# Split operands in three passes for the attention scores of the third and fourth layer

## What is computed

```
# layer 3, per block of 128 queries
z = jnp.einsum('bhqd,bhkd->bhqk', qb, k).astype(jnp.float32) * scale
strict = kpos[None, :] < tpos[:, None]
...
# layer 4: queries and keys are normalised per head and scaled by a gain
k_sh = rms_norm(split_heads(kvf[..., :HD]), shared_k_norm_g)
...
q = rms_norm(split_heads(hn @ fox_w_q[j]), fox_q_norm_g[j])
...
logits = (jnp.einsum('bhqd,bhkd->bhqk', qb, k).astype(jnp.float32) * scale
          + fb[..., :, None] - f_cum[:, :, None, :])
causal = kpos[None, :] <= tpos[:, None]
```

## Time and profile before

| | us |
|---|---|
| median of 3 runs | 1357.53 |
| lowest and highest | 1356.75, 1357.81 |
| the profiled execution | 1357.98 |
| its span, first to last instruction | 1356.2 |
| busy in it: TensorE / VectorE / ScalarE | 1340.0 / 924.8 / 795.8 |
| mean granted TensorE clock | 1.0 of full speed |

### The profile page before, as it was taken

One profiled execution on the slowest core, in us unless ns is written; L12 is line 12 of the kernel. 1 busy time (PEld: TensorE's weight loads), 2 busy tenths in 40 slices (PEclk: granted clock), 3 DMA queues, 4 the chain that ended last, 5 costly groups with the idle time before them and its releaser, 6 DMA issues.

```text
span 1356.2 us, 21057 instructions
## 1 busy us (share of the span) xinstructions
PE 1340.0 (99%) x6920; PEld 1114.2 (82%) x6920; DVE 924.8 (68%) x1679; ACT 795.8 (59%) x1478; POOL 115.4 (9%) x182
## 2 busy tenths in 40 slices
PE   8999999999999999999999999999999999999998
PEld 7887888888888888888888888888887778888887
DVE  6877666556787766665687876666677877666665
ACT  7765655546765655554686665555478766555544
POOL 5220232300000000000000000000002210000000
PEclk9999999999999999999999999999999999999999
DMA  9444787765653555655644456555645545655551
GB/s 288 150 141 136 202 226 220 222 202 177 193 152 125 158 185 186 186 186 193 208 132 152 129 162 195 186 186 186 202 156 180 164 132 156 197 189 186 186 194 54
DMA packets 177851, 239.29 MB, mean 176 GB/s; under 512 B 13532, under 2 KB 152940, under 8 KB 177787
## 3 DMA queue, kind: packets, MB, share of 16 engines
q1 hardware_dynamic: 174778, 229.41, 53.3%
q0 software_dynamic: 2976, 9.02, 3.4%
q10 hardware_dynamic: 32, 0.01, 0.0%
HBM read 237.27 MB, written 1.13 MB: 176 GB/s over the span
## 4 chain that ended last, share of the span: by engine, by line
PE 93%; DVE 4%; DMA 1%; ACT 1%; issue 1%; POOL 1%; SPq 0%; DVEq 0%; POOLq 0%; ACTq 0%
PE acc L1289 17%; PE acc L1291 16%; PE acc L1290 16%; PE sc L1291 11%; PE sc L1289 11%; PE sc L1290 11%; PE turn L1411 6%; PE turn L1491 1%; DVE wlo L918 1%; PE sc L1446 1%; PE sc L1451 1%; DVE z L995 1%; PE turn L1475 1%; DMA bias<-nfc_scratch 0%; DMA raw<-in_da_w_qkv 0%
## 5 line engine op out<-in xcount | busy, mean ns | idle before, releaser
L918 DVE SCALAR_TENSOR_TENSOR wlo<-raw,gain,whi 128x512 fp32r<-128x512 f32 (+2 forms) x680 | 442.4, 707 | 25.2 <-ACT whi L680 25.1
L680 ACT ACTIVATE whi<-raw,gain 128x512 fp32r<-128x512 f32 (+2 forms) x680 | 418.9, 681 | 31.4 <-PE acc L1291 21.3
L1289 PE MATMUL acc<-whi,xhi 128*128 128x512 f32 (+1 forms) x704 | 255.4, 363 | 1.7 <-DVE wlo L918 1.6
L1289 PE MATMUL sc<-whi,xhi 128*128 128x512 f32 x640 | 253.0, 395 | 0.0
L1291 PE MATMUL sc<-whi,xlo 128*128 128x512 f32 x640 | 249.8, 390 | 0.0
L1290 PE MATMUL sc<-wlo,xhi 128*128 128x512 f32 x640 | 249.4, 390 | 0.0
L1291 PE MATMUL acc<-whi,xlo 128*128 128x512 f32 (+1 forms) x704 | 247.4, 351 | 0.0
L1290 PE MATMUL acc<-wlo,xhi 128*128 128x512 f32 (+1 forms) x704 | 247.2, 351 | 0.0
L1289 PEld LDWEIGHTS acc<-whi,xhi 128*128 128x128 f32 x704 | 133.1, 189 | 22.9 <-issue 3.2
L1291 PEld LDWEIGHTS acc<-whi,xlo 128*128 128x128 f32 x704 | 133.0, 189 | 18.3
L1290 PEld LDWEIGHTS acc<-wlo,xhi 128*128 128x128 f32 x704 | 133.3, 189 | 15.8
(11 more groups left out here) (179 smaller groups left out, 1557.0 us busy)
## 6 DMA issues: line engine op xcount, KB each, us to landing
raw<-in_ffn_w_gu SPq DMA_DIRECT2D x176, 256.0 KB
raw<-in_ffn_w_gate SPq DMA_DIRECT2D x88, 256.0 KB
raw<-in_ffn_w_up SPq DMA_DIRECT2D x88, 256.0 KB
raw<-in_ffn_w_down SPq DMA_DIRECT2D x44, 512.0 KB
raw<-in_ffn_w_d SPq DMA_DIRECT2D x44, 512.0 KB
raw<-in_ple_w_gate SPq DMA_DIRECT2D x32, 512.0 KB
raw<-in_da_w_qkv SPq DMA_DIRECT2D x32, 256.0 KB
raw<-in_na_w_qkv SPq DMA_DIRECT2D x32, 256.0 KB
```

Source lines behind the costliest of these rows:

```text
L680: ins = act.activation(whi[:, u % RING, c0:c1], raw[:, u % RING, c0:c1], ACT.Copy, scale=scale)
L918: ins = dve.scalar_tensor_tensor(out=lo, in0=w, scalar=gain[:, g:g + 1], in1=hi.bitcast(F32), op0=ALU.mult, op1=ALU.subtract)
L1289: pe.matmul(dst, xh, wh, start=first, stop=False)
```

## The change

Layers 3 and 4 take the way of layers 1 and 2. `split_scores` and `qk32` go, and ScalarE writes the upper halves into `qkT`. VectorE gets a new step `turnqk` in both layers, which makes the lower halves and releases the bank. In layer 4, where the gains of queries and keys are applied here, VectorE does this with four multiply-subtract operations of 128x256 per group instead of two subtractions of 128x512. The step stands ahead of the weight halves of its step in layer 3, and ahead of the value eviction in layer 4.

```diff
-    L_SB: [[], [], ["evacv", "scores0"], ["scores1"], ["post0", "post1"], ["turnp0"], ["turnp1"], ["pvt*"]],
-    L_FX: [["evacqk"], ["headnorm"], ["evacv"], ["mask", "scores0"], ["scores1", "post0"], ["turnp0", "post1"], ["turnp1"],
+    L_SB: [[], ["turnqk"], ["evacv", "scores0"], ["scores1"], ["post0", "post1"], ["turnp0"], ["turnp1"], ["pvt*"]],
+    L_FX: [["evacqk"], ["headnorm"], ["turnqk", "evacv"], ["mask", "scores0"], ["scores1", "post0"], ["turnp0", "post1"], ["turnp1"],
...
-SPLIT = count([x for x in EV_LIST if x[0] in ("x", "o", "g", "side") or x[0] == "qk" and split_scores(x[1])])
+SPLIT = count([x for x in EV_LIST if x[0] in ("x", "o", "g", "side", "qk")])
...
                 elif name == "turnqk":
-                    if L == 2 and j == 0:
-                        act.wait_ge(fin_ready, T)
...
                         dst = qkT[:, :, t * P:(t + 1) * P]
-                        if split_scores(L):
-                            act.activation(dst, src, ACT.Copy).then_inc(turn_hi, 1)
-                            continue
-                        dst = qk32[:, :, t * P:(t + 1) * P]
                         if L == L_FX:
                             act.activation(dst[:, 0:2], src[:, 0:2], ACT.Copy, scale=gain[:, GAIN_Q:GAIN_Q + 1])
-                            ins = act.activation(dst[:, 2:4], src[:, 2:4], ACT.Copy,
-                                                 scale=gain[:, GAIN_K:GAIN_K + 1])
+                            act.activation(dst[:, 2:4], src[:, 2:4], ACT.Copy, scale=gain[:, GAIN_K:GAIN_K + 1])\
+                                .then_inc(turn_hi, 1)
                         else:
-                            ins = act.activation(dst, src, ACT.Copy)
-                        ins.then_inc(turn_out[e % 2], 1)
+                            act.activation(dst, src, ACT.Copy).then_inc(turn_hi, 1)
...
-                        lo_half(("qk", L, j, t), qklo[at], qkT[at],
-                                tb[e % 2][:, :].rearrange("p (k c) -> p k c", k=4), e)
+                        src = tb[e % 2][:, :].rearrange("p (k c) -> p k c", k=4)
+                        if L != L_FX:
+                            lo_half(("qk", L, j, t), qklo[at], qkT[at], src, e)
+                            continue
+                        dve.wait_ge(turn_hi, SPLIT[("qk", L, j, t)])
+                        for b, g in ((0, GAIN_Q), (2, GAIN_K)):
+                            ins = dve.scalar_tensor_tensor(out=qklo[at][:, b:b + 2], in0=src[:, b:b + 2],
+                                                           scalar=gain[:, g:g + 1],
+                                                           in1=qkT[at][:, b:b + 2].bitcast(F32), op0=ALU.mult,
+                                                           op1=ALU.subtract)
+                        ins.then_inc(turn_out[e % 2], 1)
...
-                        if not split_scores(L):
-                            for q in range(2):
-                                ins = pe.matmul(dst[q], qk32[rows[q], b, tile], qk32[rows[q], 2 + b, 0:kk], start=True,
-                                                stop=True)
-                            continue
                         for n, (x, y) in enumerate(((qkT, qkT), (qkT, qklo), (qklo, qkT))):
```

More of the change, by code:

```diff
@@ L124, in keys @@
     return P if L >= L_SB and t == 0 else S
-def split_scores(L):
-    return L < L_SB
 def p_blocks(L, t):
@@ L257, in build @@
         fin_gain = sb("fin_gain", [P, D])
-        qk32 = fin_gain[:, :].rearrange("p (k c) -> p k c", k=4)
         ident = sb("ident", [P, P])
```

## The result

Over eight executions each, taken in turn on one chip, the changed kernel takes 1361.88 us in the median (1360.99 to 1363.0) and the kernel before 1357.73 (1356.75 to 1358.58): a ratio of 1.0031, 95% interval 1.0023 to 1.0040, so 4.15 us slower. The profiled execution of the changed kernel took 1361.53 us (span 1359.7), 3.5 us more than that of before. The forecast was 1358.7 us with a range up to 1361.2; the time lies above the range.

The account below looks back on a forecast made before the run. TensorE's own instruction stream, 99% busy, was taken as the bound. Blocks +0.2 us and waits 0.15 + 0.3 + 0.6 = +1.05 us gave +1.2 us, so 1358.7 us on the median; range 1356.7 to 1361.2 with rivals.

Parts of the forecast that it names:

- the block prices: TensorE's score blocks: each t=0 block 0.2 us more, each t=1 block 0.16 us less; five groups counted, +0.2 us.
- The t=1 block: Score block of the second query tile, 256 key columns: from 1.38 to 1.22 us, 0.16 us less each.
- The t=0 step: Time between split pairs at 128 columns in the first query tile's scores: 0.11 us, bounds 0.06 and 0.21.
- the rival by columns: Columns set the t=0 step, 0.06 us, or no new waits: 1357.8 us, without the waits 1356.7; chance 0.15.
- that by the plain product's price: Narrow t=0 split products cost a plain product's 0.21 us per step: 1360.8 us, up to 1361.5; chance 0.13.
- the waits in layer 3's group 0: TensorE waits about 0.15 us for VectorE's lower halves before the third layer's first scores.
- none in its groups 1 to 3: Third layer: a VectorE idle gap of 3.47 us hides the 1.2 us of new work; no cost.
- layer 4's group 1: VectorE's new 1.6 us fit in 1.81 us of idle time ahead of the output's lower half; no cost.
- group 2: Fourth layer: value eviction 2.5 us late; after idle gaps TensorE's softmax transposes come 0.6 us later.
- Group 3 ... nothing reaches TensorE: Fourth layer: the same 2.5 us lateness is taken by idle gaps before the score evictions; no cost.
- layer 4's group 0: VectorE's 1.6 us meet 1.18 us of idle time for a DMA; t=1 scores start 0.3 us later.
- The third rival: VectorE becomes the bound in layer 4, 1.6 us per group, 6.4 in all: 1363.5 us; chance 0.09.

Follow-up runs that it names:

- t0_narrow: Changed kernel with the t=0 score products' moving columns cut from 128 to 64 in layers 3 and 4, half those scores left out; 1361.27 us, one execution.
- v_first: Changed kernel with VectorE evicting the values ahead of the lower halves in layer 4; 1360.13 us, 1.0019 of the kernel before.
- after_pad: Changed kernel with sixteen idle 16x16 products added at the program's start; 1360.29 us, 1.0018 of the kernel before.
- the repeat: Changed kernel run again unaltered: 1361.03 us, 1.0025. Where 2.3 is given: kernel before with sixteen idle start products, run again, 1360.03 us, 1.0015.
- before_pad14: Kernel before with fourteen idle 16x16 products added at the program's start; 1359.87 us, 1.0014 of the kernel before.
- after: The changed kernel itself, scores split in layers 3 and 4, against the kernel before; 1361.88 us, ratio 1.0031.
- v_pad: Changed kernel with value eviction ahead of the lower halves in layer 4 and sixteen idle products at the start; 1358.55 us, 1.0005 of the kernel before.
- l3_pad: Kernel with scores split in layer 3 alone, plus sixteen idle products at the start; 1358.22 us, 1.0005 of the kernel before.
- l3_only: Changed code with scores split in layer 3 alone, layer 4 keeping plain products; 1360.19 us, 1.0016 of the kernel before.

## Why the prediction was wrong

**Right: the block prices.** The t=1 block went from 1.38 to 1.22 us, as read off the second layer. The t=0 step is 0.11 us, taken from how fast weight loads followed each other, and t0_narrow bears out that columns don't set it. The blocks balance, as forecast: eight times about +0.17 and -0.16 (+0.2 was forecast for t=0, which makes five times 0.04 us; measured is five times 0.01). Its first step is 0.13 us, not 0.22. Neither the rival by columns nor that by the plain product's price happened.

**Right: the waits in layer 3's group 0** (0.15 forecast, 0.20 measured), none in its groups 1 to 3, nothing lost in layer 4's group 1, and 0.56 us in group 2 (0.6 forecast). Two slips are of no weight: of the three waits on L1033 in the earlier trace rows two lie in group 0 and one in group 1, none in group 2 (0.04 us in the sum), and 1357.5 + 6.4 is 1363.9, not 1363.5.

**The step that failed: "Group 3 ... nothing reaches TensorE".** I saw that VectorE's value eviction came 2.5 us late, and followed its lateness only to the score evictions behind it. The eviction has a reader of its own. It frees the accumulator banks that the output projection writes, and in the last group the output projection comes in the same step. TensorE waits 0.85 us for it, and that product starts 1.0 us later against its neighbours than before; the group loses 1.1 us. v_first, which evicts the values first, takes it away.

**The second step that failed: layer 4's group 0, forecast +0.3 us.** VectorE's own part is right (0.56 and 0.55 against 0.40 and 0.39 us in after_pad). But I took the DMA that ended VectorE's idle time as fixed. It starts with a store whose landing depends on what else is in the DMA engines, and there the change put a packet that I take for TensorE's code. With it the wait is 1.49 us, or 2.14 in the repeat. In the traces this is 0.9 us (1.49 against 0.56 in after_pad), 1.6 in the repeat and 1.9 in before_pad14 (2.31 against 0.40). The medians give 1.6 (after against after_pad), 0.7 (the repeat against it), and 1.8 to 2.3 for the kernel before with 16 or 14 products.

**The sum.** Forecast +1.2. With group 3's 1.1 it is 2.3; after_pad measured 1360.29 - 1357.72 = 2.6. With the late store's 0.9 it is 3.2 for the profiled execution, which lost 3.55 (0.17 of it ahead of the third layer's scores); with 1.6 it is 3.9, and the medians gave 4.15, or 3.4 in the repeat. With both causes taken out (v_pad) 0.8 us are left over the kernel before; its trace has 0.38 of them in layer 3 and 0.31 in group 0 of layer 4. The third rival, VectorE as the bound in layer 4, didn't happen: VectorE's lateness counts only where something waits for it, by 0.3, 0, 0.65 and 1.1 us in the four groups and not by 1.6 in each. v_pad and l3_pad, 0.8 and 0.5 us above the kernel before, aren't told from it by their intervals: the split as such costs little, and a gain isn't seen.

**Open.** The two held-up packets end 0.4 to 0.9 us after the others, but the store's landing is 1.0 to 1.5 us later than without a code packet; where the rest goes no trace shows. Nor does one say on which DMA engine a packet ran, and that the packets are TensorE's code is read from their rhythm alone. Both profiles of the kernel with sixteen products are of executions near 1357.1 us; that those near 1360 are like before_pad14's is an inference, not seen, and so it is for l3_only's slower ones.

## What to carry to other kernels

When an instruction in the middle of an engine's queue becomes late, list all who wait for each instruction behind it, the one that frees a bank as well as the one that delivers data; the reader that comes soonest decides, and it may be another one in the last turn of a loop. Added instructions also move the 16 KB packets that I take for the engine's code; where a short DMA round trip stands on the critical path, a change of one or two us can come from there, and idle instructions elsewhere, in several numbers (here 14 and 16 met the store and 18 and 22 didn't), tell it from the change's own cost. The three-pass product paid at 256 columns (0.16 us less a block) and cost 0.17 us more at 128, where its step stayed at 0.11 us.

## What was not expected of the hardware

The time of this kernel moves by 2 us with the number of instructions ahead of one 16 KB store: 14 idle products at the start cost 2.1 us and 16 cost 1.8 (2.3 in the repeat), while 18 or 22 cost nothing that the intervals show. The packet's place doesn't follow in even steps either (1045.8 us with none, 1035.2 with 14, 1036.9 or 1036.1 with 16, 1036.5 with 18, 1030.5 with 22), so it can't be placed by counting records alone.

TensorE's clock can answer a wait. In v_first, which had waited 0.50 us up to 1041.49 and 1.97 us up to 1047.29, the stretches of TensorE right behind it (us; PE, PEld, DVE, ACT and POOL busy, granted clock, DMA share, GB/s):

```profile
1047.00:1048.00 1.00, 0.71 (x11) 0.74 (x12) 0.93 (x6) 0.43 (x3) 0.00 (x0) 1.00 0.58 206
1048.00:1049.00 1.00, 1.00 (x8) 0.70 (x5) 1.00 (x3) 1.00 (x6) 0.00 (x0) 0.73 0.04 12
1049.00:1050.00 1.00, 1.00 (x4) 0.77 (x3) 1.00 (x6) 1.00 (x5) 0.00 (x0) 0.50 0.00 0
...
1051.00:1052.00 1.00, 1.00 (x4) 0.77 (x4) 0.98 (x2) 1.00 (x5) 0.00 (x0) 0.56 1.00 355
1052.00:1053.00 1.00, 1.00 (x9) 0.83 (x7) 1.00 (x4) 1.00 (x6) 0.00 (x0) 1.00 0.12 40
```

The granted clock falls to 0.50, that is 1.2 in place of 2.4 GHz, from about 1048.5 to 1052, and four matmuls start in a microsecond. In before_pad14, with one wait of 2.31 us at the same place, it stayed at 1.00, so the length of the wait alone doesn't decide it.
